# Second mixer's attention units laid between its query and key chunks, and the output projections' weight quarters taken by rows

## The reference, cut to what matters

```python
def moba_mixer(h, w_in, w_out, rel_table):      # S = 256 = one block, 8 heads of 128
    q, k, v = split(h @ w_in, 3)
    s_own = (q @ k.T) * dh ** -0.5 + bias_own    # bias by distance, per head
    s_own = where(dist_own >= 0, s_own, -inf)
    p = softmax(s_own)
    o = p @ v                                    # per head
    return o @ w_out                             # 1024 x 1024
```

## Time and profile before

| | |
|---|---|
| median of 3 runs (lowest to highest) | 1731.88 us (1731.41 to 1732.63) |
| the profiled execution's own time | 1731.59 us |
| its span in the trace | 1729.8 us |
| mean granted TensorE clock | 0.989 of full |
| PE busy | 1686.8 us, 98% of the span |
| DVE busy | 938.9 us, 54% |
| ACT busy | 720.4 us, 42% |
| POOL busy | 58.8 us, 3% |

### The profile page before, as it was taken

How to read it: one execution, slowest core, us unless ns; L and a number is a source line. 1 busy time by engine, 2 the same in 40 slices (tenths; PEclk the granted TensorE clock), 3 DMA queues, 4 the chain that set the end, 5 groups by cost and what they waited for, 6 DMA issues and landing times.

```text
span 1729.8 us, 26204 instructions
## 1 busy us (share of the span) xinstructions
PE 1686.8 (98%) x11476; PEld 1535.9 (89%) x11484; DVE 938.9 (54%) x928; ACT 720.4 (42%) x822; POOL 58.8 (3%) x72
## 2 busy tenths in 40 slices
PE   8998999999899999999999999999999999999999
PEld 6987899989789998899989799998999987689998
DVE  5476545455554445645476654555454586754444
ACT  5404433443543434433353443435443334743432
POOL 0023000000000000000000000000000020000000
PEclk8999999999999999999999999999999998999999
DMA  9543555557436465545455465556654535036461
GB/s 289 188 75 120 183 171 198 168 179 235 146 107 215 155 218 171 196 169 204 162 185 193 156 207 185 193 178 193 215 191 175 176 121 171 2 120 213 155 218 74
DMA packets 221650, 297.16 MB, mean 172 GB/s; under 512 B 7403, under 2 KB 184767, under 8 KB 221536
## 3 DMA queue, kind: packets, MB, share of 16 engines
q1 hardware_dynamic: 215256, 284.39, 49.1%
q10 hardware_dynamic: 6280, 11.09, 2.8%
HBM read 291.27 MB, written 3.15 MB: 170 GB/s over the span
## 4 chain that ended last, share of the span: by engine, by line
PE 89%; DVE 5%; ACT 3%; DMA 2%; issue 1%; SPq 0%; ACTq 0%; DVEq 0%
PE ps L1672 20%; PE ps L1570 16%; PE ps L1573 16%; PE ps L1571 16%; PE ps L1592 3%; PE ps L1586 3%; PE ps L1587 3%; DVE wlo L1054 2%; PE ps L1625 2%; PE ps L1627 2%; PE ps L1626 2%; ACT whi L623 1%; DMA raw<-in_hgrn_w_out 1%; PE ps L1608 1%; PE ps L1950 1%
## 5 line engine op out<-in xcount | busy, mean ns | idle before, releaser
L1054 DVE TENSOR_TENSOR wlo<-raw,whi 128x2048 fp32r<-128x2048 f32 (+2 forms) x270 | 602.5, 2251 | 240.0 <-ACT whi L623 239.4
L1570 PE MATMUL ps<-xhi,whi 128*128 128x256 f32 x2432 | 599.4, 284 | 2.8 <-DVE xlo L1080 2.8
L1571 PE MATMUL ps<-xhi,wlo 128*128 128x256 f32 x2432 | 598.2, 283 | 0.0
L623 ACT ACTIVATE whi<-raw 128x2048 fp32r<-128x2048 f32 (+1 forms) x265 | 498.0, 1900 | 105.7 <-DMA raw<-in_hgrn_w_out 40.6
L1570 PEld LDWEIGHTS ps<-xhi,whi 128*128 128x128 f32 x2432 | 467.7, 192 | 5.4 <-issue 3.3
L1571 PEld LDWEIGHTS ps<-xhi,wlo 128*128 128x128 f32 x2432 | 468.0, 192 | 2.2
L1573 PE MATMUL ps<-xlo,whi 128*128 128x256 f32 x2432 | 342.2, 283 | 0.0
L1573 PEld LDWEIGHTS ps<-xlo,whi 128*128 128x128 f32 x2432 | 314.5, 192 | 0.0
L689 ACT ACTIVATE hhi<-hid 128x512 fp32r<-128x512 f32 x54 | 34.1, 632 | 512.1 <-DVE hid L1118 461.1
L1118 DVE TENSOR_TENSOR hid<-silu,ps 128x512 f32<-128x512 f32 x60 | 41.3, 688 | 320.6 <-PE ps L1573 320.6
L1672 PE MATMUL ps<-whi,hhi 128*128 128x512 f32 x480 | 187.5, 391 | 0.0
(11 more groups left out here) (221 smaller groups left out, 1334.7 us busy)
## 6 DMA issues: line engine op xcount, KB each, us to landing
raw<-in_ffn_w_gate_up SPq DMA_DIRECT2D x80, 1024.0 KB, 5.6
raw<-in_ffn_w SPq DMA_DIRECT2D x62, 1024.0 KB, 5.5
raw<-in_ffn_w_down SPq DMA_DIRECT2D x44, 1024.0 KB, 5.7
raw<-in_hgrn_w_in SPq DMA_DIRECT2D x16, 1024.0 KB, 5.7
raw<-in_moba_w_in SPq DMA_DIRECT2D x12, 1024.0 KB, 5.3
raw<-in_conv_w_in SPq DMA_DIRECT2D x10, 1024.0 KB, 5.2
raw<-in_ffn_w_gate_up SPq DMA_DIRECT2D x16, 512.0 KB, 5.0
raw<-in_kv_w SPq DMA_DIRECT2D x6, 1024.0 KB, 5.0
```

Of the source, the lines that this page charges most:

```text
L623: act.activation(whi[s % WRING][:, 0:width], raw[n % RING][:, 0:width], ACT.Copy).then_inc(split_hi, 1)
L1054: ins = dve.tensor_tensor(wlo[s % WRING][:, part], raw[n % RING][:, part], whi[s % WRING][:, part].bitcast(F32), ALU.subtract)
L1570: pe.matmul(out, hi[:, k, tile], xhi[:, k, :], start=k == 0, stop=False)
L1571: pe.matmul(out, lo[:, k, tile], xhi[:, k, :], start=False, stop=False)
```

## The change: what it does

1. **moba, PE.** The units of the attention are laid between the q and k chunks: q1, logits 0, k1, transposes 0, q2, values 0, logits 1, k2, transposes 1, q3, values 1, logits 2, k3, transposes 2, logits 3. Then the projection's quarter 0, values 2, transposes 3, quarter 1, values 3, quarters 2 and 3. All logits go to banks 2 and 3, so logits u+1 wait for the maxima of unit u. No warming matmuls are left in it.
2. **moba, ACT and DVE.** Their queues take the same steps of a unit in between the splits of the chunks, in an order written out by hand. The split of `out` 2 and 3 comes after the last exponentials and after the last transposes.
3. **moba, where the output goes.** The first pair's output goes to `hhi`, `hlo`, as `xhi` and `xlo` are still being read by k chunks; the others go to `xhi`, `xlo` as before.
4. **All mixers, the output projection.** Quarters 0 and 1 are now the left and right columns of the upper 512 rows, 2 and 3 those of the lower. So quarters 0 and 1 need only the first half of the mixer's output. A bank holds (column half, tile) in another order. Nothing of the sum is complete halfway; tile 0's two halves come at the end of its part of quarter 2 and of quarter 3. DVE and ACT split both first chunks of the next stage before the additions; tile 1's left half is added after tile 0's norm.
5. **hgrn.** Three warming matmuls stand before k = 2 of quarter 0 alone, not at k = 4 and 6.

```diff
             def out_product(name):
                 for n in range(4):
-                    load(quarter(out_w[name], n % 2, n // 2 * 512), name, "out", n)
+                    load(quarter(out_w[name], n // 2, n % 2 * 512), name, "out", n)
...
             # ACT, after a mixer's output projection
-                split(after, "first", 0)
-                squares(after, 0, 0)
+                for n in range(2):
+                    split(after, "first", n)
+                for half in range(2):
+                    squares(after, 0, half)
                 squares(after, 1, 0)
-                split(after, "first", 1)
-                bound(after, early=True)
+                x_high(after, 0)
+                squares(after, 1, 1)
+                x_high(after, 1)
...
             # ACT, moba
                 for i in range(4):
+                    if i >= 2:
+                        keep_probs(i - 2)
+                    if i < 3:
+                        split(name, "q", i + 1)
+                    else:
+                        split(name, "out", 0)
+                    keep(0, i)
+                    if i == 2:
+                        y_high(0, 1, *moba_out(0, hhi, xhi))
+                    if i < 3:
+                        split(name, "k", i + 1)
+                    else:
+                        split(name, "out", 1)
+                    if i >= 1:
+                        exps(i - 1)
+                    keep(1, i)
+                y_high(1, 2, *moba_out(1, hhi, xhi))
+                keep_probs(2)
+                exps(3)
                 split(name, "out", 2)
+                y_high(2, 3, *moba_out(2, hhi, xhi))
+                keep_probs(3)
                 split(name, "out", 3)
-                attention(HEADS // 2, 1, moba_out)
+                y_high(3, 4, *moba_out(3, hhi, xhi))
...
             # DVE, after a mixer's output projection
-                split(after, "first", 0)
-                dve.wait_ge(chunk_used, chunks.number[name, "out", 1] + 1)
-                add(0, 0)
-                add(1, 0)
-                split(after, "first", 1)
-                dve.wait_ge(tile_summed, MIXERS.index(name) + 1)
-                add(0, 1)
+                for n in range(2):
+                    split(after, "first", n)
+                for half in range(2):
+                    dve.wait_ge(tile_summed, 2 * MIXERS.index(name) + half + 1)
+                    add(0, half)
                 normalise(after, 0)
-                dve.wait_ge(chunk_used, chunks.number[name, "out", 3] + 1)
-                add(1, 1)
+                for half in range(2):
+                    dve.wait_ge(chunk_used, chunks.number[name, "out", 2 + half] + 1)
+                    add(1, half)
                 x_low(after, 0)
...
             # DVE, moba
-                for i in range(1, 4):
-                    split(name, "q", i)
-                    split(name, "k", i)
-                for n in range(4):
-                    split(name, "out", n)
+                split(name, "q", 1)
+                split(name, "k", 1)
+                split(name, "q", 2)
                 dve.wait_ge(bias_landed, 32)
-                attention(HEADS // 2, 1, moba_out, lambda u: mbias[:, 2 * u:2 * u + 2, :], P ** -0.5)
+                for u in range(3):
+                    if u == 1:
+                        moba_low(0)
+                    moba_max(u)
+                    if u < 2:
+                        split(name, "k", u + 2)
+                    else:
+                        split(name, "out", 1)
+                    scale_probs(u)
+                    if u < 1:
+                        split(name, "q", 3)
+                    elif u < 2:
+                        split(name, "out", 0)
+                moba_low(1)
+                moba_max(3)
+                split(name, "out", 2)
+                scale_probs(3)
+                moba_low(2)
+                split(name, "out", 3)
+                moba_low(3)
...
             # PE, output projection
+            def out_first(name, n, pieces=4, sums=False, first=None):
+                hi, lo = weights(name, "out", n, k=4)
+                for k in range(4):
+                    if sums and n == 0 and k == 2:
+                        keep_warm(3, bank=3)
+                    if n == 0 and k % (KT // pieces) == 0:
+                        pe.wait_ge(ylo_ready, at.y + k // (KT // pieces) + 1)
+                    for t in range(TT):
+                        mm = out_part(name, n, t, k, hi, lo, first)
+                used(mm, name, "out", n)
...
             # PE, moba
+                def score(u):
+                    if u == 0:
+                        pe.wait_ge(v_kept, 4)
+                    else:
+                        pe.wait_ge(max_ready, at.att + u)
+                    for r in range(2):
+                        pe.wait_ge(bank_free[r], moba_base[r] + u + 1)
+                    logits(u, 2, ...)
+                project(0, 0)
+                project(1, 0)
+                for u in range(3):
+                    project(0, u + 1)
+                    if u >= 1:
+                        value(u - 1)
+                    score(u)
+                    project(1, u + 1)
+                    turn_probs(u)
+                score(3)
+                freed[0], freed[1] = moba_base[0] + 4, moba_base[1] + 4
+                out_first(name, 0, first=(hhi, hlo))
+                value(2)
+                turn_probs(3)
+                pe.wait_ge(max_ready, at.att + 4)
+                out_first(name, 1, first=(hhi, hlo))
+                value(3)
+                at.att += 4
+                out_last(name, first=(hhi, hlo))
```

More of the change, by code:

```diff
@@ L56 @@
 WARM_FINAL = 12
[L57 removed]
+WARM_NSA = (12, 0)
 WARM_CMP = 16
@@ L807, in attention @@
                     if i < units:
[L808 to L820, removed]
+                        exps(i, scale)
                     if i >= 2 and (i - 1) % branches == 0:
-                        act.wait_ge(pv_done, at.att + i - 1)
-                        dst, src = pair_out((i - 2) // branches)
-                        act.activation(dst(xhi), src, ACT.Copy).then_inc(yhi_ready, 1)
+                        pair = (i - 2) // branches
+                        dst, src = pair_out(pair)
+                        y_high(pair, i - 1, dst(xhi), src)
                     if 0 <= i - 1 < units:
[L827 to L830, removed]
+                        keep_probs(i - 1)
                 at.att += units
@@ new lines, in out_part @@
+            def out_part(name, n, t, k, hi, lo, first):
+                kk = 4 * (n // 2) + k
+                tile = slice(t * P, (t + 1) * P)
+                out = ps[:, 2 * (n % 2) + t, :]
+                high, low = first if first and kk < 2 else (xhi, xlo)
+                pe.matmul(out, high[:, kk, tile], hi[:, k, :], start=kk == 0, stop=False)
+                pe.matmul(out, high[:, kk, tile], lo[:, k, :], start=False, stop=False)
+                return pe.matmul(out, low[:, kk, tile], hi[:, k, :], start=False, stop=kk == KT - 1)
@@ L1647, in out_product, with out_last @@
+            def out_last(name, pieces=4, first=None):
+                after = FOLLOWS[name]
+                parts = [weights(name, "out", n, k=4) for n in (2, 3)]
                 for t in range(TT):
@@ L1793, in hgrn @@
                     mm.then_inc(o_ready, 1)
-                at.y += 4
-                out_product(name, sums=True)
-            def attention(pairs, branches, q_of, k_of, pv, masked=False, warm=(0, 0)):
+                free(3)
+                keep_warm(8, bank=3)
+                out_first(name, 0, sums=True)
+                pe.wait_ge(heads_summed, 3)
+                for t in range(TT):
+                    mm = pe.matmul(ps[:, 4, t:t + 1], gq[:, 0, t * P:(t + 1) * P], one, start=True, stop=True)
@@ new lines, in hgrn, with logits @@
+                mm.then_inc(o_summed, 1)
+                out_first(name, 1)
+                out_last(name)
+            def logits(u, first_bank, q, k, masked=False):
+                if masked:
+                    for a in range(2):
+                        pe.matmul(ps[:, first_bank + a, 0:3 * P], ident_b[:], mask_b[:], start=True, stop=False,
+                                  skip_group_check=True)
+                for part, tile, keys in ((slice(0, P), slice(0, P), slice(0, P)), (slice(P, 3 * P), slice(P, S), slice(0, S))):
+                    for a in range(2):
+                        mm = pe.matmul(ps[:, first_bank + a, part], q[a][:, tile], k[a][:, keys],
+                                       start=not masked, stop=not masked or part.stop == 3 * P, skip_group_check=masked)
+                mm.then_inc(scored, 1)
@@ new lines, in turn_probs, with values @@
+            def turn_probs(u):
+                pe.wait_ge(probs_ready, at.att + u + 1)
+                if u >= 1:
+                    pe.wait_ge(pt_ready, at.att + u)
+                for a in range(2):
+                    for n in range(3):
```

(7 more changed lines are left out.)

239 lines of the change are left out of this document (109 added, 130 removed).

## The result

The changed kernel takes **1717.3 us** in the median of four runs (1714.15 to 1719.34), the kernel before beside it 1732.26 (1731.41 to 1733.37). The ratio is 0.991, 95% interval 0.9898 to 0.9922.

What follows compares the result with a forecast made beforehand. PE bounds the kernel, busy 98% of the span, so only its idle or needless work and the clock count. Moba -8.7, hgrn -1.3, three tails +0.45 give -9.55 us: 1722.0, median 1722.3, range 1718.8 to 1727.

Steps and rivals of the forecast that it cites:

- The walk through moba: moba's four queues stepped through: q1 to the next stage 77 us instead of 85.7, gain 8.7.
- rivals C and E: moba: C, transposes 0 to 2 wait, 1725.3 or 1726.8, chance 0.15; E, such waits bring clock falls, 1733.0, chance 0.03.
- rival D: moba's projection: weights of `out` 1, 2 and 3 come late, 6 to 9 us come back, 1728 to 1731; chance 0.05.
- PE idles 2.7 us: moba, before transposes 3: PE waits 2.7 us for DVE's scaling, which stands behind the split of `out` 2.
- The turn waits 1.2 us: moba's tail: late splits of the next stage's first chunks delay tile 0's additions and norm, 1.2 us.
- 0.8 us before the first product: moba's tail: `x_high` stands behind the square of tile 1's left half, 0.8 us before the next stage's first matmul.
- The clock, 1.45 us behind that idle, in one mixer: moba: the new 2.7 us idle brings one fall to half clock, costing 1.45 us, bounds 0 and 3.0.
- Rival B: moba: no clock fall at the 2.7 us idle, 1720.9; without the tail's 2.0 us too, 1718.9; chance 0.15.
- Before, the fall lay under a wait: Old moba order: the clock fall after 4.04 us without work lay under a wait for transposes.
- hgrn's six matmuls, 1.3 us: hgrn's projection: six warming matmuls fewer at 0.215 us each, gain 1.3 us, as nothing is waited for there.
- 0.15 us in each of three other tails: hgrn, conv, nsa: tile 1's left addition and square before `x_high` cost 0.15 us each, bounds 0 and 0.5.
- below it nothing in the sum could go: Whole kernel: the low end of the range is rival B's 1718.9, with neither clock fall nor the tail's 2.0 us.

Runs made afterwards that it cites:

- scale_first: Changed kernel with DVE's scaling of moba's last unit ahead of the split of `out` 2: 1713.2 +- 1.1 us; again 1716.1 +- 0.6.
- xhigh_first: Changed kernel with the next stage's high part of tile 0 ahead of the square of tile 1's left half on ACT: 1719.2 +- 0.8 us.
- before_warm: Kernel before with 24 warming matmuls instead of 6 in moba's idle before the third unit's logits: 1731.3 +- 0.7 us.
- rows_only: Changed kernel with moba's attention put back as before; projections' order, order after them and hgrn's fewer warming matmuls stay: 1730.7 +- 0.9 us.
- tail_early: Changed kernel with scale_first's and xhigh_first's edits, and moba's split of the next first chunk ahead of the last output parts: 1717.1 +- 0.5 us; again 1715.1 +- 0.4.
- after_warm: Changed kernel with twelve matmuls on zeros in moba's idle before the last transposes: 1717.5 +- 1.0 us.
- filled: tail_early with 9 more warming matmuls ahead of hgrn's projection and 9 ahead of conv's: 1712.5 +- 0.4 us.

## Why the prediction was wrong

The sign, the mechanism and the mixer's size in the two profiles compared were right; the total was not. By its own steps:

- **The walk through moba.** q1 to the next stage 77.0 us (forecast 77), the gain 8.8 (8.7). That both agree so closely is in part luck. The sum has 5.1 us of waits, and the list above has 3.4, with the clock's 1.6 for 1.45; so PE's own work took some 1.5 us more than the sum gives it. It is spread over many small pieces (chunk k1, between logits and transposes, takes 5.96 us from start to start, where a chunk was put at 5.76), and no run takes it apart. It is luck too that these two executions were compared: moba takes 97.3, 98.2 and 98.0 us in the three unfilled profiles of the old order and 88.5, 88.5 and 86.9 in those of the new, a mean gain of 9.9. Transposes 0 to 2 and logits 3: no wait, where margins of 0.2 were given; rivals C and E are out. ACT loads its table once, and the loads move without a wait; rival D is out.
- **"PE idles 2.7 us" before the last transposes:** 2.45, by the steps named. Shown by scale_first, which removes it.
- **The turn waits 1.2 us:** 0.42. The walk had too much here by 0.8. **0.8 us before the first product:** 0.53; xhigh_first gives 0.7 for its cause.
- **The clock, 1.45 us behind that idle, in one mixer.** The size is right: 1.6, three times (88.5 against 86.9 in moba, 25.5 against 23.9 in hgrn, 24.4 against 22.8 in conv). That it falls each time is not: with the same idle it fell in two profiles and not in two. Rival B and the forecast aren't two outcomes of the kernel but two of its executions. The Trainium skill (TensorE: Matmul & The Clock Gate, What's actually happening) says that where the gate's count begins varies from run to run. The traces here agree (2.45 us with a fall, 2.44 without).
- **"Before, the fall lay under a wait".** Right for the profile of before (97.3, filled 97.2), and not for every execution: 98.0 and 98.2 in two others.
- **hgrn's six matmuls, 1.3 us.** Right where both executions have the fall in the projection (26.8 against 25.5); 2.8 against those of the new code without it.
- **0.15 us in each of three other tails.** Not there: conv's projection takes 24.4 or 22.8 in old and new code alike, and nsa's 22.7 to 22.8. The cost is seen in moba alone; in hgrn the tail isn't measured apart from the six matmuls.

**The step that failed** is the total: "The profiled execution took 1731.59, so 1722.0", and with it "below it nothing in the sum could go". It took everything outside the edits as the same in every execution, and priced the clock at one new idle of moba, although showed a fall in another mixer. In the two profiles compared, the start and hgrn's levels differ by 2.7 us, which the sum has at nothing: 92.2 against 91.3, and 99.9 against 96.8 less the 1.3 of the edit. Of this, 0.3 is the shorter wait for weights and the rest goes with the falls (three and one in the start, one and none in the levels); for the start, whose length differs by 1.5 us between profiles with one fall each, that is argued and not shown. With moba's 8.8 and hgrn's 1.3 that gives the 12.4 of the spans, but for rounding. The remaining 2.0 to the median is that three of the four runs had a higher clock than the profiled one: 1719.34 at 0.992, 1717.54 and 1717.06 at 0.993, 1714.15 at 0.996. At one clock the difference is 10.0 to 11.3, nearer to the sum's 9.55 than the 15 of the first result.

**Open.** The 16 runs of the changed kernel have a mean clock of 0.9921, the 60 of before 0.9893; the spread within a kernel is too small for this to be chance alone. Part of it is moba, where falls under waits are gone: filling them in the old order (before_warm) raised the clock to 0.9909, without time. What holds it up further, worth about 1.5 us (1.2 +- 0.7 thousandths by 1.21), isn't settled, and chance isn't excluded for it. rows_only, with the same hgrn, is at 0.9891, so it is not plainly hgrn's edit; tail_early is at 0.9900 and after_warm at 0.9930 with the same code ahead of moba. Repeats of one version had the same number of falls in hgrn (after 1, 1, 1; scale_first 1, 1; tail_early 3, 3), those of the old code 2 and 3. Whether edits shift the falls for a whole program, or executions on one occasion share them (the experiments ran on three occasions, each on another chip), these runs can't tell. Open too is whether the new order of the quarters shortens the wait for hgrn's weights, worth up to 1.0 us on average; no run changes that alone.

## What to carry to other kernels

When the traces of a kernel show falls behind several idles of TensorE (here those of 2 us and more), its total is a draw: put the clock's share into the range (here 1.6 us for each idle that may or may not have a fall), and compare kernels stage by stage, in more than one profile of each, before an edit of 1 or 2 us is judged. When the parts of a forecast agree with a trace, check the terms too: here waits too long and work too short cancelled. In a walk of two in-order queues, look where an engine stands idle for a split that waits for another engine while ready work is behind it: one exchanged pair of lines was worth 2.5 us and the fall that followed. Matmuls on zeros in an idle that can't be removed don't shorten the wait, but in the four places tried here the clock stayed up behind them.

## What the runs showed of the hardware

- The same kernel ran from 1714.2 to 1723.6 us, and 84% of the variance within the kernels (-0.92 squared) goes with the mean granted clock.
- A PE idle of 2.44 or 2.45 us was followed by a granted clock of 0.57 in some executions and 1.00 in others; one of 2.09 us ahead of hgrn's projection had a fall behind it in nine profiles (0.61 in after) and none in four. Each fall cost 1.6 us where PE set the pace, nothing under a wait, and 0.9 where it outlasted one.
- With the idle filled by matmuls on zeros the clock stayed at 1.00 in all four stretches looked at (moba in after_warm and before_warm, hgrn's and conv's projections in filled). Unfilled, the falls came in two of four, three of three, nine of thirteen and nine of thirteen profiles.
